# Decoder step on one core: attention scores from rounded high and low parts, a scan whose decays come from cumulative logs, and its end products moved from GpSimd to ScalarE

## The reference, cut to what matters

```python
cum = jnp.cumsum(log_a.astype(f32).reshape(b, n, c, h), axis=2).swapaxes(2, 3)
seg = jnp.exp(jnp.where(causal, cum[..., :, None] - cum[..., None, :], -jnp.inf))
scores = jnp.einsum('bnihd,bnjhd->bnhij', q, k) * seg
y_intra = jnp.einsum('bnhij,bnjhe->bnihe', scores, v)
k_end = k * jnp.exp(cum[..., -1:] - cum).swapaxes(2, 3)[..., None]
chunk_kv = jnp.einsum('bnjhd,bnjhe->bnhde', k_end, v)
```

```python
s = (einsum('bqhd,bkhd->bhqk', qn, k_nope) + einsum('bqhr,bkr->bhqk', qr, kr)) * MLA_SCALE
s = jnp.where(kpos[None, :] <= qpos[:, None], s, -jnp.inf)
p = jax.nn.softmax(s, axis=-1)
```

## Time and profile before

| | |
|---|---|
| median of three runs | 2322.02 us |
| the profiled execution, and its span | 2319.74 us, 2318.1 us |
| granted TensorE clock, mean | 0.996 |
| PE, PE weight load, DVE, ACT, POOL busy | 98%, 95%, 48%, 34%, 7% |
| hybrid phase | about 402 to 867 us of the span |
| attention phase | about 1626 to 1937 us |

### The profile page before, as it was taken

The page is one execution under the profiler, slowest core; times in us unless marked ns, Lnnn a source line. Parts: engine busy times, 40 slices in busy tenths (PEclk is TensorE's granted clock), DMA queues, the critical chain, the costliest instruction groups (busy, mean ns, idle before and its releaser), DMA issues.

```text
span 2318.1 us, 49263 instructions
## 1 busy us (share of the span) xinstructions
PE 2278.5 (98%) x19770; PEld 2210.2 (95%) x19770; DVE 1114.9 (48%) x1770; ACT 799.6 (34%) x1411; POOL 172.2 (7%) x239
## 2 busy tenths in 40 slices
PE   9999999999999999999999999999999999999998
PEld 9999999998788999999999999999987799999997
DVE  4444334776536544444334444433557645444433
ACT  4332233554324433323333333233344334222322
POOL 0000001021100010000010000001114411000000
PEclk9999999999999999999999999999999999999999
DMA  4232334232333332323333333333446733333333
GB/s 145 91 90 90 100 101 112 74 104 83 100 142 104 91 96 87 90 90 90 105 101 87 93 93 90 100 101 98 153 150 219 270 98 88 95 91 90 95 101 105
DMA packets 119619, 249.46 MB, mean 108 GB/s; under 512 B 15233, under 2 KB 15377, under 8 KB 118145
## 3 DMA queue, kind: packets, MB, share of 16 engines
q1 hardware_dynamic: 105552, 193.05, 28.2%
q0 software_dynamic: 13792, 54.43, 6.8%
q10 hardware_dynamic: 144, 0.09, 0.0%
HBM read 237.30 MB, written 9.95 MB: 107 GB/s over the span
## 4 chain that ended last, share of the span: by engine, by line
PE 92%; DVE 5%; issue 1%; ACT 1%; DMA 0%; POOLq 0%; SPq 0%; DVEq 0%; POOL 0%; ACTq 0%
PE psum L355 82%; PE psum L2282 2%; PE psum L2327 1%; PE psum L1127 1%; PE psum L1051 1%; PE psum L2319 1%; DVE w_low L333 1%; PE psum L2375 1%; PE psum L2251 1%; PE psum L2225 1%; DVE conv_sum L1536 0%; PE psum L2269 0%; PE psum L1114 0%; PE psum L999 0%; PE psum L1130 0%
## 5 line engine op out<-in xcount | busy, mean ns | idle before, releaser
L333 DVE TENSOR_TENSOR w_low<-w_raw,w_high 128x512 fp32r<-128x512 f32 x718 | 511.4, 731 | 643.4 <-ACT w_high L327 642.8
L355 PE MATMUL psum<-x_high,w_high 128*128 128x260 f32 x3840 | 773.3, 283 | 7.6 <-DVE w_low L333 4.7
L355 PE MATMUL psum<-x_low,w_high 128*128 128x260 f32 x3840 | 770.1, 282 | 0.0
L355 PE MATMUL psum<-x_high,w_low 128*128 128x260 f32 x3840 | 768.9, 281 | 0.0
L355 PEld LDWEIGHTS psum<-x_high,w_high 128*128 128x128 f32 x3840 | 588.3, 188 | 12.9 <-DVE w_low L333 3.4
L355 PEld LDWEIGHTS psum<-x_low,w_high 128*128 128x128 f32 x3840 | 591.3, 188 | 0.0
L355 PEld LDWEIGHTS psum<-x_high,w_low 128*128 128x128 f32 x3840 | 590.5, 188 | 0.0
L327 ACT ACTIVATE w_high<-w_raw 128x512 fp32r<-128x512 f32 x718 | 433.6, 623 | 451.6 <-PE psum L355 435.9
L355 PE MATMUL psum<-hidden_high,w_low 128*128 128x260 f32 x1408 | 284.0, 283 | 0.0
L355 PE MATMUL psum<-hidden_high,w_high 128*128 128x260 f32 x1408 | 282.9, 282 | 0.0
L355 PE MATMUL psum<-hidden_low,w_high 128*128 128x260 f32 x1408 | 282.9, 282 | 0.0
(11 more groups left out here) (387 smaller groups left out, 1743.9 us busy)
## 6 DMA issues: line engine op xcount, KB each, us to landing
w_raw<-in_weights_dram SPq DMA_DIRECT2D x720, 256.0 KB, 2.7
cache_pages<-in_cache_pages_dram POOLq DMA_DIRECT2D x128, 272.0 KB, 4.2
ret_sample_state<-in_state_ret_dram POOLq DMA_DIRECT2D x2, 2048.0 KB, 7.5
out_ret_s_dram<-ret_sample_state POOLq DMA_DIRECT2D x2, 2048.0 KB, 6.6
out_y_dram<-residual SPq DMA_DIRECT2D x8, 260.0 KB, 2.2
ssm_sample_state<-in_state_ssm_dram POOLq DMA_DIRECT2D x2, 1024.0 KB, 5.5
out_ssm_s_dram<-ssm_sample_state POOLq DMA_DIRECT2D x2, 1024.0 KB, 4.5
residual<-in_x_dram SPq DMA_DIRECT2D x3, 520.0 KB, 6.3
```

What stands on the lines that cost most here:

```text
L333: nc.vector.tensor_tensor(WL[:, slot, :], WRAW[:, slot, :], WH[:, slot, :].bitcast(F32), ALU.subtract).then_inc(w_split, 1)
L355: mm = nc.tensor.matmul(PS[:, b0 + 2 * m + half, 0:cols], w, x[:, half * cols:(half + 1) * cols], start=start, stop=stop)
```

## The change

Three sets of edits, in one diff (cut; lines that are only "..." leave out).

1. The scan. The cumulative logs of all four chunks are made once by eight small fp32 matmuls in the middle of `hin(1)`, split in a high and a low part, and brought by eight transfers into rows `CUR`. Per chunk, 4 fp32r matmuls of 512 columns replace the 8 of `ssm_scores`, and 8 (4 data, 4 mask) the 16 of `ssm_decays`. `masked_logs` and `chunk_logs` go, `choices` (10 ACT operations, once) and `cum_highs` come. `chunk_end` moves from POOL to ACT, one operation for each head.
2. The order of the work: in the last convolution group `a.splits(1)` stands ahead of `conv_tile`; `state_decay(0)`, the scaling of x by d, a pair of splits in the chunks, and the rotary key's copies in the attention phase move.
3. The scores of attention: queries and keys of a head are split by ACT (`score_highs`) and DVE (`score_lows`), PE makes three fp32r passes for each fp32 matmul. ACT takes 1024 of the 1280 columns of the copy L2718. The splits of the next weights, in whose places the parts lie, move from turns 2 to 5 to turns 14 to 16.

```diff
@@ PE, scan
-            pe.wait_ge(law_done, c + 1)
-            for h8 in range(8):
-                mm = nc.tensor.matmul(... LAW[:, h8] ..., UPTO, start=True, stop=True)
+            if c:
+                pe.wait_ge(sst_done, c)
+            else:
+                acquire(pe, step)
+                pe.wait_ge(cur_loaded, 16 * 2 * NTT)
+            for half in range(2):
+                for g in range(2):
+                    nc.tensor.matmul(PS[:, b + 2 + half, :], SEL[...], CUR[0:64, ... 512], start=g == 0, stop=g == 1)
...
-            for h in range(SH):
-                mm = nc.tensor.matmul(... LM[:, h, :], UPTO, start=True, stop=True)
+            for q in range(4):
+                nc.tensor.matmul(PS[:, b + q, :], CUM[:, c, :], CUR[:, q * 512:(q + 1) * 512], start=True, stop=False)
+            for q in range(4):
+                mm = nc.tensor.matmul(PS[:, b + q, :] ..., NGH[:], IDH[:] ... broadcast, start=False, stop=True)
...
+        def cumulative_logs(k):
+            if k != 6:
+                return
+            wait_free(pe, "ssm xT0")
+            for c in range(NTT):
+                for q in (2, 3):
+                    mm = nc.tensor.matmul(PS[32 * q:32 * q + 32, b, c * P:(c + 1) * P], LA[...], UPTO, start=True, stop=True)
+            mm.then_inc(cum_full, 1)
...
-        hin(1)
+        hin(1, before_k=cumulative_logs)
+        pe.wait_ge(cum_read, 1)
@@ ACT, scan
-        def masked_logs(c):
+        def chunk_end(c):
             if c:
-                wait_full(act, ("ssm D", c - 1))
+                wait_full(act, ("ssm y", c - 1))
+            else:
+                act.wait_ge(xr_loaded, 16 * 24)
             for h in range(SH):
-                ins = nc.scalar.activation(LM[:, h, :], AFTER, ACT.Copy, scale=LA[:, c, h:h + 1])
-            ins.then_inc(l_done, 1)
+                ins = nc.scalar.activation(XEND[:, own], XTOK[:, c, own], ACT.Copy, scale=DEX[...])
+            ins.then_inc(xend_done, 1)
...
             if g == 0:
-                masked_logs(0)
+                choices()
...
-        act.wait_ge(xd_done, 1)
-        nc.scalar.activation(XH8[:], XDS[:], ACT.Copy).then_inc(xh8_done, 1)
         for t in range(8):
             ins = nc.scalar.activation(XS[:, t, :], XS[:, t, :], ACT.Copy, scale=...)
+        act.wait_ge(xd_done, 1)
+        nc.scalar.activation(XH8[:], XDS[:], ACT.Copy).then_inc(xh8_done, 1)
@@ DVE, scan
         for m in range(2):
+            a.splits(1)
             conv_tile(20, m)
-            a.splits(1)
...
-            nc.vector.tensor_tensor(CS[:], BC[...], CS[:], ALU.mult).then_inc(free(step), 1)
-            wait_free(dve, step)
+            nc.vector.tensor_tensor(SM[:], PS[:, b:b + 2, 0:P], UPTO ..., ALU.mult).then_inc(free(step), 1)
+            nc.vector.tensor_tensor(CS[:], BC[...], CS[:], ALU.mult).then_inc(cs_done, 1)
+            dve.wait_ge(cs_done, c + 1)
+        state_decay(0)
         a.splits(2)
         chunk_scores(0)
...
-            a.splits(2)
-            if c == 0:
-                state_decay(0)
+            if c % 2:
+                a.splits(2)
             if c % 2 == 0:
                 step = ("ssm outer", k)
                 wait_full(dve, step)
                 nc.vector.tensor_tensor(SSS[:], SSS[:], PS[:, bank0(step):bank0(step) + 4, :], ALU.add).then_inc(free(step), 1)
                 wait_free(dve, step)
+                a.splits(2)
@@ attention
+            pe.wait_ge(qkl_done, h + 1)
...
                 n, (bank, col) = (it + 1) * P, s_place[it]
-                nc.tensor.matmul(..., Q[:, h, it * P:n], KTT[:, h, 0:n], start=True, stop=False)
+                nc.tensor.matmul(out, high[:, 0, it * P:n], high[:, 1, 0:n], start=True, stop=False)
+                nc.tensor.matmul(out, low[:, 0, it * P:n], high[:, 1, 0:n], start=False, stop=False)
+                nc.tensor.matmul(out, high[:, 0, it * P:n], low[:, 1, 0:n], start=False, stop=False)
...
+        def score_highs(h):
+            nc.scalar.activation(QKH[h % 2][:, 0, :], Q[:, h, 0:NP_], ACT.Copy)
+            nc.scalar.activation(QKH[h % 2][:, 1, :], KTT[:, h, :], ACT.Copy).then_inc(qkh_done, 1)
...
+        def probs_turned(h):
+            wait_full(act, step)
+            nc.scalar.activation(PT[:, 0:512], PS[:, b, :], ACT.Copy)
+            act.wait_ge(pt_done, h + 1)
+            nc.scalar.activation(PT[:, 512:1024], PS[:, b + 1, :], ACT.Copy).then_inc(free(step), 1)
...
             if h < NCK:
                 sample_exps(h)
+            if h < MH - 2:
+                score_highs(h + 2)
+            if h < MH:
+                probs_turned(h)
...
-            if 2 <= h < 2 + R:
-                a.splits(1)
+            if h >= MH - 2:
+                a.splits(2 if h == MH - 1 else 1)
...
+        def score_lows(h):
+            dve.wait_ge(qkh_done, h + 1)
+            nc.vector.tensor_tensor(QKL[h % 2][:, 0, :], Q[:, h, 0:NP_], high[:, 0, :], ALU.subtract)
+            nc.vector.tensor_tensor(QKL[h % 2][:, 1, :], KTT[:, h, :], high[:, 1, :], ALU.subtract).then_inc(qkl_done, 1)
...
                 link(nc.vector.reciprocal(RL[:, h % 2, :], LS[:, h % 2, :]))
+            if h < MH - 2:
+                score_lows(h + 2)
             step = ("att TO", h)
             wait_full(dve, step)
...
-                ins = nc.vector.tensor_copy(PT[:], ... 1280)
+                nc.vector.tensor_copy(PT[:, 1024:1280], PS[:, b + 2, 0:256]).then_inc(pt_done, 1)
```

More of the change, by code:

```diff
@@ L1062, in out @@
                 return PS[64 * (h % 2):64 * (h % 2) + 64, b + h // 8, (t % 4) * P:(t % 4 + 1) * P]
-            wait_free(pe, ("ssm sc", c))
+            pe.wait_ge(cs_done, c + 1)
             if c:
@@ L1395, in act @@
             a.splits(2)
-            if c < NTT - 1:
-                masked_logs(c + 1)
+            chunk_end(c)
             a.splits(2)
@@ L1945, in pool @@
         pool.wait_ge(convs_done, XBC + 1)
+        pool.sem_inc(cum_place_free, 1)
         pool.dma_start(SSS[:], io["state_ssm"][:, 0:4]).then_inc(sss_loaded, 16)
+        pool.wait_ge(cum_read, 1)
+        for c in range(NTT):
+            for part in range(2):
+                pool.dma_start(CUR[32 * part + c:32 * part + c + 1, :],
+                               CUM[64 + 32 * part:64 + 32 * part + SH, c, :]).then_inc(cur_loaded, 16)
         pool.wait_ge(rows_ready, 1)
@@ L2077, in mla_parts @@
     KRT = at("rotary_key", [P, T], ZONE + 24960)
+    ring = [e.WH_OFF + 4 * CW * ((plan.first[("wo", 0)] + 2 * u) % R) for u in range(2)]
+    QKH = [at(f"score_parts_high{u}", [P, 2, NP_], ring[u], F32R) for u in range(2)]
+    QKL = [at(f"score_parts_low{u}", [P, 2, NP_], ring[u] + 4 * CW * R, F32R) for u in range(2)]
     small = [ZONE + 27648]
@@ L2273, in scores @@
             step = ("att S", h)
-            acquire(pe, step)
-            if h == 0:
+            if h:
+                acquire(pe, step)
+            else:
+                pe.wait_ge(v_half, 2)
+                pe.wait_ge(v_third, 2)
                 wait_free(pe, ("uk", 3))
                 pe.wait_ge(krr_done, 6)
-                pe.wait_ge(masks_done, 1)
             b = bank0(step)
+            pe.wait_ge(qkl_done, h + 1)
+            high, low = QKH[h % 2], QKL[h % 2]
             for it in S_ORDER:
                 n, (bank, col) = (it + 1) * P, s_place[it]
-                nc.tensor.matmul(PS[:, b + bank, col:col + n], Q[:, h, it * P:n], KTT[:, h, 0:n], start=True, stop=False)
+                out = PS[:, b + bank, col:col + n]
+                nc.tensor.matmul(out, high[:, 0, it * P:n], high[:, 1, 0:n], start=True, stop=False)
+                nc.tensor.matmul(out, low[:, 0, it * P:n], high[:, 1, 0:n], start=False, stop=False)
+                nc.tensor.matmul(out, high[:, 0, it * P:n], low[:, 1, 0:n], start=False, stop=False)
+                if h == 0 and it == S_ORDER[0]:
+                    pe.wait_ge(masks_done, 1)
                 mm = nc.tensor.matmul(PS[:, b + bank, col + it * P:col + n], IDR[:], NGR[:], start=False, stop=True)
@@ L2433, in act @@
             b = bank0(step)
+            nc.scalar.activation(V[:, 0:2, g * 512:(g + 1) * 512], PS[:, b:b + 2, :], ACT.Copy).then_inc(v_half, 1)
+            if g == 0:
+                act.wait_ge(krr_done, 6)
+                wait_free(act, ("uk", 3))
+                wait_free(act, ("uq", 7))
+                score_highs(0)
             if g:
@@ L2717, in dve @@
             if h < MH:
-                ins = nc.vector.tensor_copy(PT[:], PS[:, b:b + 3, :].rearrange("p a n -> p (a n)")[:, 0:1280])
-            ins.then_inc(free(step), 1)
-            wait_free(dve, step)
+                nc.vector.tensor_copy(PT[:, 1024:1280], PS[:, b + 2, 0:256]).then_inc(pt_done, 1)
+            else:
+                ins.then_inc(free(step), 1)
+                wait_free(dve, step)
             if h < NCK - 2:
                 sample_probs_by_key(h)
-            if 2 <= h < 2 + R:
-                a.splits(1)
+            if h >= MH - 2:
+                a.splits(2 if h == MH - 1 else 1)
```

112 lines of the change are left out of this document (69 added, 43 removed).

## The result

Twenty executions of each kernel: the changed kernel takes 2325.39 us in the median (2321.95 to 2328.74), the one before 2322.32 (2319.41 to 2325.43). The ratio is 1.0016, 95% interval 1.0010 to 1.0023: +3.1 to +3.7 us, where the forecast had -2.9. The measured time lies inside the range, but the change goes the other way.

What follows compares the result with a forecast made beforehand. PE was taken to bound the kernel, with 92% of the chain that ended last. From the profiled 2319.74 us, scan -12.9 and attention +10.3 gave 2317.1, or 2319.4 against the median; range 2308 to 2329.

Steps and rivals of the forecast that it cites:

- The pace of a matmul: PE's matmuls: fp32 of 128 columns 0.223 us each, fp32r of 512 columns 0.232; 2.8 us less work per scan chunk.
- (b): Scan, hin(1): the eight new fp32 matmuls pair on two column groups and cost 0.9 us, 1.8 if they do not.
- The turn: Attention head loop: PE waits for the low parts, a turn takes 8.9 us, +0.72 for 13 heads, 9.4 together.
- The entry: Attention, first heads: scores(0) starts on partial reads, scores(1) waits for the same queue, -0.2 us; head 2 pays +1.8.
- The rotary key: Ahead of the attention loop: five small operations move behind the reciprocal, PE's wait falls from 2.36 to 0.4 us, -3.0.
- Turns 14, 15 and behind the loop: Attention's end: turn 14 has no wait, -0.35 us; later splits and copies delay the first wo matmul, +2.7.
- The scan: The four chunks: less matmul work and shorter waits, minus new charges, sum to -12.9 us, between -9 and -16.
- (c): Scan: ACT scales x before rounding the sample rows, so 24 transfers start near 512.4 instead of 508.6, landing at 526.9.
- the clock falls in the loop: Rival, head loop: waits bring the lower clock, a turn is 9.9 us, +13, total 2332; chance 0.12.
- ACT is late in every chunk: Rival, scan: ACT's 16 operations also delay chunks 1 to 3, up to 1.5 us each, total 2324; chance 0.08.
- The move of the split costs nothing: Rival, scan: the split ahead of conv_tile(20) costs zero, hin(1) starts 0.85 early, -3.5 us more, total 2316; chance 0.13.
- The first rival: Head loop: the parts come in time, PE stays the bound, 15 turns give -5.3 us, total 2303; chance 0.12.

Runs made afterwards that it cites:

- run 7: Changed kernel with ScalarE's roundings ahead of the next head's exponentials and VectorE's subtractions right behind its maxima; 2307.89 us, ratio 0.9942.
- run 8: run 7 plus chunk 0's end products on GpSimd and head 1's subtractions behind the copies of the samples' queries; 2304.17 us, ratio 0.9929.
- run 10: Kernel before with the attention's edits except the split parts, scores still fp32 matmuls; 2318.32 us, ratio 0.9990.
- run 2: Attention's part of the change alone, scan of the kernel before; 2336.85 us, ratio 1.0065.
- run 1: Scan's part of the change alone, attention of the kernel before; 2309.48 us, ratio 0.9956.
- run 3: Changed kernel with ScalarE's two roundings of head h+2 ahead of the samples' exponentials instead of behind; 2309.09 us, ratio 0.9946.
- run 9: Changed kernel with VectorE's subtractions behind its reads of the turned probabilities, lengthening the loop's wait on purpose; 2347.32 us, ratio 1.0116.
- run 6: Changed kernel with the weight splits again behind the last convolution group's tiles on VectorE; 2326.08 us, ratio 1.0016.
- run 5: Changed kernel with chunk 0's end products made by one GpSimd operation, as before; 2324.88 us, ratio 1.0015.

## Why the forecast was wrong, step by step

The forecast had -12.9 for the scan and +10.3 for the attention. The profiles have -9.6 (the mean below) and +14.4: the first is 3.3 short, the second 4.1, and together they are a little more than the 6.0 between -2.9 and +3.1. Both halves failed, the scan by one unwritten term and the attention by two mis-sized ones.

**The pace of a matmul** held for L1064, four of which take 0.92 where the clock is full. The four of L1062 take 1.13 to 1.2 and those of L1047 1.13, where 0.93 was summed: 0.4 to 0.5 more in each chunk, of which the chunks' waits hide a part. The eight matmuls of (b) take 1.07 (forecast 0.9), so they do pair.

**The turn** was right in its mechanism and its chain (4.14 against 4.17). Mis-sized was one term: "Twelve fp32r matmuls take ... 1.77 to 1.9, the four masks 0.11 each as now: 2.2 to 2.35, 0.35 less". The block takes 2.48 even where nothing waits (1751.30 to 1753.78 in run 7), 0.16 less than before and not 0.35. So a turn is 9.09, not 8.9: +2.4 in 13 turns.

**The entry** is the step that failed in the attention: "`scores(1)` waits for the same queue as before: -0.2". Head 1's two subtractions stand on VectorE ahead of the copies of the samples' queries, PE waits 0.90 for these, and behind that wait it ran at the lower level: `scores(1)` takes 3.8 instead of 2.6. Behind the wait of 2.10 for head 2, which the forecast had (2.1), `scores(2)` takes 4.1 for the same reason. I had 1.6 for heads 0 to 2 together; it is 4.7. This is no matter of one execution: in every profile that has the wait of 0.9 the lower level follows it, and in run 8, which moves the subtractions and takes the parts earlier, neither is there and the entry is 5.4 shorter.

**The rotary key** held: -3.0 forecast, -3.5 measured, with PE's wait at 0.4 as forecast (the earlier trace rows before, 2.36). Behind it the clock stayed at 1.00 (1654.70 to 1659.50), so all of the 1.6 came back and not the 1.0 that was counted:

```profile
1654.73 0.72 PE L2216 MATMUL psum<-latent_variance,constants 1*128 1x260 f32 x8 [0.42 <-ACT latent_variance L2469]
```

**Turns 14, 15 and behind the loop** together were forecast at +2.3; 1.5 were measured, much as in run 10.

**The scan** was forecast at -12.9; alone it is -10.2, and -6.6 in the changed kernel's profile. Here is the start of L1098 in each chunk (L1073 in the old scan), in all profiled executions whose scan is that of one of the two kernels, with PE's wait for ScalarE in chunk 0 and the granted clock of 529.00 to 545.20:

| profile | chunk 0 | 1 | 2 | 3 | wait | clock |
|---|---|---|---|---|---|---|
| before | 529.23 | 557.69 | 580.75 | 605.20 | none | 0.89 |
| run 2 | 531.67 | 560.09 | 583.15 | 607.62 | none | 0.94 |
| run 10 | 529.50 | 557.92 | 580.98 | 605.45 | none | 0.89 |
| changed | 532.45 | 557.89 | 577.51 | 599.00 | 3.4 | 0.68 |
| run 1 | 530.19 | 551.68 | 571.31 | 594.32 | 1.5 | 1.00 |
| run 3 | 530.57 | 553.66 | 573.32 | 596.15 | 1.6 | 0.89 |
| run 7 | 532.21 | 553.75 | 573.41 | 596.45 | 3.4 | 1.00 |
| run 9 | 531.05 | 554.12 | 573.77 | 596.51 | 1.6 | 0.89 |

The means of the last five differ from the means of the first three by +1.2, -4.4, -7.8 and -9.6; forecast were +1.5, -6.0, -9.6 and -12.9. Run 1 meets the first three against the kernel before (+1.0, -6.0, -9.4). The step that failed is the tacit one: the 2.8 saved per chunk and chunk 1's -6.0 were summed as if PE ran at full clock behind every wait. It does not: from chunk 0 to 1 are 21.5 at full clock, 23.1 in two executions and 25.4 in one. From chunk 2 to 3 are 21.5 in the changed kernel (clock 1.00 from 577.00 to 599.00) and 22.7 to 23.0 in the others (0.90 in run 1, 577.00 to 594.30). Each of the five pays in one of the two stretches or in both. With 21.5 in both, run 1 would be at -12.4, my estimate from the table; so the forecast's other steps hold within 0.5.

**The late transfers** of (c) came near their forecast (first issue 511.9, forecast 512.4) for another reason than the one given. ScalarE's order costs 0.3; VectorE hands the sample rows over 3.1 later than before. That the number fits is luck.

**Of the rivals**, "the clock falls in the loop" did not come at a wait of 0.92: the clock is 1.00 over all 13 turns. The Trainium skill (TensorE: Matmul & The Clock Gate, HAM oscillation) describes a loop in which PE waits 3 to 5 us for a transfer in every turn and starts every turn throttled. The waits here are shorter, and a fall in every turn was not seen: none in 13 turns at 0.92, four in 13 turns at 2.12. "ACT is late in every chunk" fell: it is waited for in chunk 0 alone. "The move of the split costs nothing" fits the medians of run 6, but its profile has the move cost something, less than was charged. The first rival, that the parts come in time, is false for this order of the queues; in run 3, with two lines moved, it is true.

**Left open.** Why the last small transfer lands 2.0 after its issue in run 1 and 3.9 in the changed kernel (3.8 in run 7); the weights' transfers run at the same time in both. And what decides whether the lower level follows a wait: it came with the 3.4 us in the changed kernel and not in run 7. The theory (D) that this wait brings it fell with run 7, which has the wait and full clock, and with run 5, which has no wait and still the lower level in chunk 1.

## What to carry to other kernels

An operation added to an engine with idle time costs its place in the queue, not its length: follow its input back through the other engines' queues, and put it where its input is ready and its buffer free, not where its consumer stands (runs 3, 7 and 9). Where a change shortens PE's work, sum the gain with a part lost to the lower clock behind each wait that stays. And one profiled execution can miss a stage by 4 us, as that of the changed kernel did for the scan: before a stall is blamed, look at it in a second profile with the same code.

## What was not expected of the hardware

- A wait of the same length, at the same place of the same code, came with either level. This is run 7, its wait ahead of L1098 and the window over it:

```profile
532.21 1.08 PE L1098 MATMUL psum<-ssm_x_end,ssm_b_tokens 128*64 128x512 f32 x4 [3.38 <-ACT ssm_x_end L1364]
533.09 1.95 PE L1104 MATMUL psum<-ssm_weights,ssm_x_tokens 128*64 128x128 f32 x32
```

```profile
529.00:545.20 16.20, 10.87 (x90) 8.90 (x91) 8.37 (x11) 7.71 (x19) 0.57 (x1) 1.00 0.29 97
```

  After 3.42 in the changed kernel the same 32 matmuls took 3.43, in a window of 0.68.
- The lower level was more regular in one place than in another. It followed the wait of 0.9 in the entry in every profile that has this wait, and the wait of 1.83 ahead of L1062 in chunk 1 in six of the nine profiles with the new scan (L1062 and L1064 behind it take 2.12 together at full clock in run 1, and 3.5 in the changed kernel and in run 5).
- In a block of three fp32r passes at full clock the first pass takes longer than the others: from its start to the second pass were 0.31, 0.23 and 0.17 us (512, 384 and 256 columns), for the second and third 0.23, 0.17 and 0.12. The block takes 2.48 instead of the 2.33 that the shorter paces make (run 7, 1751.30 to 1753.78).
- 16 ScalarE operations of 128x64 with a scale per partition took 3.93 us, 0.245 each, where no row of the kernel before showed one of that width; the estimate from wider ones had been 3.8.
